# Delta rule: when the SP queue fetches the attention channels, and when the ACT queue fetches the bias bands

## The chip, the cores and the metric
The kernel runs on one NeuronCore of a Trainium2 chip. The metric is the device time of one execution in microseconds (us). Five engines take part: TensorE (PE: matmuls, and its weight loads, PEld), VectorE (DVE), ScalarE (ACT), GpSimd (POOL) and SyncE (SP), which here only issues DMAs. The core has 16 DMA engines. DMAs that SP issues run on queue q1, those that ACT issues on queue q10.

## The reference
One decoder block over 2048 tokens of width 1024. What matters here is the gated delta rule of four heads (width 128), which runs over the sequence in chunks, and the attention that follows it:

```python
def step(state, inp):
    u0_c, w_c, qg_c, kg_c, aqk_c, gl_c = inp
    u = u0_c - jnp.einsum("bhck,bhkv->bhcv", w_c, state)
    o = jnp.einsum("bhck,bhkv->bhcv", qg_c, state) + jnp.einsum("bhij,bhjv->bhiv", aqk_c, u)
    state = gl_c[..., None, None] * state + jnp.einsum("bhck,bhcv->bhkv", kg_c, u)
    return state, o
...
# attention, three dilations
s = jnp.einsum("brnqhd,brnkhd->brnhqk", qb, kk) * (dh ** -0.5)
s = s + bias.transpose(2, 0, 1)
```

A chunk's state needs the state of the chunk before, so the chunks run one after another. Around these two parts stand a conditioned norm, one projection, an output projection, a router, 32 experts and a final norm.

## The kernel before
The program runs phase by phase: projection of tokens, projection of channels (with the products of every chunk of the delta rule, stored to DRAM), `deltanet` (16 chunks of 128 tokens; stage D below), `attention`, output and routing, experts, final norm. Between phases all engines meet at a barrier. The change is in `deltanet` alone.

In `deltanet` each engine runs its own loop over the chunks, and semaphores tie the loops together. Per chunk c:

- **SP** (`load_solve`, `store`, `load_z`, `load_chain`). In turn c of its loop it issues, strictly in this order: `load_solve(c + 2)`, that is one load of `nt` (256 KB) and eight small block loads into `dz` and `dzt` (16 KB each, in rows of 128 bytes); `store(c - 1)`, which waits for `y_out_ready`, the last step of POOL for chunk c - 1; `load_z(c + 1)`; `load_chain(c + 2)`, five loads of 256 KB (`kc`, `vb`, `kg`, `qg`, `aqk`); and then, in turns 0 to 7, one attention channel block, `m.qk[:, c, :]` (1 MB, from `ch_d` into `big`, L1064). Nobody in this stage reads that block. The attention reads it after the barrier.
- **PE** runs `read_state(c)`, `sixth_z(c)`, `fifth_y(c + 1)`, `solved(c)`, `fifth_z(c + 1)`, `outputs(c)`, `sixth_y(c + 1)`. `fifth_y(c + 1)` waits for `nt_in` and `d_in`, the landing of all nine loads of `load_solve(c + 1)`. `solved(c)` gives `u` of chunk c.
- **ACT** copies `u` out of PSUM (L1186), squares and copies the outputs, and takes a root. In turns 2, 3 and 4, before all that, it issues one bias band for the attention (`bias[:, c - 2, :, :]`, 1 MB in rows of 1 KB, L1181). Nobody in this stage reads that either. ACT waits for the three bands at the stage's end.
- **DVE** masks, subtracts and forms the next state. After the next state of chunk c it runs `reciprocals(c - 1)`.
- **POOL** scales the output; its last step for chunk c - 1 waits for `reciprocals(c - 1)` and releases SP's `store(c - 1)`.

The copy of `u` on ACT happens once for each chunk. The text calls its start U(c) and uses it as the clock of the stage.

Of the kernel before, what the change touches and what calls it, by code (L numbers as in the profile page):

```python
# [11 lines left out]
P = 128  # L12
T = 2048
NT = T // P
# [9 lines left out]
NCONV = 3 * GH  # L24
AH = 8
# [3 lines left out]
NB = len(BR)  # L29
BIAS_W = 384  # L30
# [133 lines left out]
def row_bc(ap, n, offset=0):  # L164

    return bass.AP(ap.tensor, ap.offset + offset, [[0, P], [1, n]])
# [290 lines left out]
def small_blocks(ap, row0, b):  # L457

    return bass.AP(ap.tensor, ap.offset + (row0 + b) * SB * SB, [[SB, SB], [P // SB * SB * SB, GH], [1, SB]])
# [495 lines left out]
def deltanet(nc, m, a):  # L955
# [5 lines left out]
    with Room(nc, "gd") as R:  # L961
# [15 lines left out]
        gain_in, later_in, zeroed, eps_set = R.sig("gain_in", 16), R.sig("later_in", 16), R.sig("zeroed"), R.sig("eps_set")  # L977
# [6 lines left out]
        bias = m.bias[:, :].rearrange("p (n h k) -> p n h k", n=NB, h=AH)  # L984
        bias_in = R.sig("bias_in", 16)
# [5 lines left out]
        def h4(ap):  # L991
            return ap.rearrange("p (h n) -> p h n", h=GH)

        def hs(h):
            return slice(h * P, (h + 1) * P)
# [3 lines left out]

        L5, L6 = C_L5, C_L6  # L1000
        BL = 2 * (P // SB)

        with R.block() as block:
            @block.sync
            def _(sp):
                def load_solve(c):
                    b = c % 2
                    if c >= 2:
                        sp.wait_ge(*y_done.n(2 * (c - 1)))
                    sp.dma_start(nt[b][:, :], m.nt_d[c]).then_inc(*nt_in[b].inc)  # L1010
                    if c >= 2:
                        sp.wait_ge(*dd_ready.n(c - 1))
                        sp.wait_ge(*dt_ready.n(c - 1))
                    else:
                        sp.wait_ge(*zeroed.n(2))
                    for k in range(P // SB):
                        s = slice(k * SB, (k + 1) * SB)
                        sp.dma_start(h4(dz[b][s, :])[:, :, s], small_blocks(m.xb_d, c * GH * P // SB, k)).then_inc(*d_in[b].inc)
                        sp.dma_start(h4(dzt[b][s, :])[:, :, s], small_blocks(m.xtb_d, c * GH * P // SB, k)).then_inc(*d_in[b].inc)

                def load_chain(c):
                    b = c % 2
                    if c >= 2:
                        sp.wait_ge(*ks_done.n(c - 1))
                        sp.wait_ge(*r_ready.n(c - 1))
                    if c:
                        sp.dma_start(h4(kc[b][:, :]), m.ch_d[GH:2 * GH, :, c * P:(c + 1) * P].rearrange("c p n -> p c n")).then_inc(*k_in[b].inc)
                    sp.dma_start(vb[:, b, :], m.vb_d[c]).then_inc(*vb_in[b].inc)
                    if c >= 2:
                        sp.wait_ge(*ds_done.n(c - 1))  # L1030
                    sp.dma_start(kg[:, b, :], m.kg_d[c]).then_inc(*kg_in[b].inc)
                    if c >= 2:
                        sp.wait_ge(*o_done.n(c - 1))
                    sp.dma_start(qg[:, b, :], m.qg_d[c]).then_inc(*qg_in[b].inc)
                    sp.dma_start(aqk[:, b, :], m.aqk_d[c]).then_inc(*aqk_in[b].inc)

                def load_z(c):
                    b = c % 2
                    if c >= 2:
                        sp.wait_ge(*y_out_ready.n(c - 1))  # L1040
                    sp.dma_start(z[:, b, :], m.z_d[c]).then_inc(*z_in[b].inc)

                def store(c):
                    b = c % 2
                    sp.wait_ge(*y_out_ready.n(c + 1))
                    sp.dma_start(m.y_d[c], o[:, b, :]).then_inc(*out[b].inc)

                sp.dma_start(gain[:, :], row_bc(a["gdn_norm"], P)).then_inc(*gain_in.inc)
                load_chain(0)
                load_solve(1)  # L1050
                load_chain(1)
                load_z(0)
                load_z(1)
                for c in range(NT):
                    if c + 2 < NT:
                        load_solve(c + 2)
                    if c >= 1:
                        store(c - 1)
                        if c + 1 < NT:
                            load_z(c + 1)  # L1060
                    if c + 2 < NT:
                        load_chain(c + 2)
                    if c < m.NCH - NCONV:
                        sp.dma_start(m.qk[:, c, :], m.ch_d[NCONV + c]).then_inc(*later_in.inc)  # L1064
                store(NT - 1)
                sp.wait_ge(*later_in.n(m.NCH - NCONV))
                for b in range(2):
                    sp.wait_ge(*out[b].n(NT // 2))
# [27 lines left out]
            def _(pe):  # L1096
# [5 lines left out]
                def fifth_y(c):  # L1102
                    b = c % 2
                    if c:
                        pe.wait_ge(*nt_in[b].n((c + 1) // 2))
                        pe.wait_ge(*d_in[b].n((c + 1) // 2 * BL))

# [63 lines left out]
            @block.scalar  # L1171
            def _(act):
                act.wait_ge(*eps_set.n(1))
                nc.scalar.activation(nrm[:, :, :], m.ssq[:, :, :], ACT.Sqrt, bias=eps[:, :]).then_inc(*nstd_ready.inc)
                act.wait_ge(*nrm_ready.n(2))
                for c in range(NT):
                    b = c % 2
                    if 2 <= c < 2 + NB:

                        src = bass.AP(m.bias_d.tensor, (c - 2) * AH * P * BIAS_W + P - 1, [[BIAS_W - 1, P], [P * BIAS_W, AH], [1, 2 * P]])  # L1180
                        act.dma_start(bias[:, c - 2, :, :], src).then_inc(*bias_in.inc)  # L1181
                    act.wait_ge(*u_done.n(c + 1))
                    if c >= 2:
                        act.wait_ge(*ds_done.n(c - 1))
                        act.wait_ge(*o_done.n(c - 1))
                    nc.scalar.copy(u[:, b, :], ps[:, U, :]).then_inc(*u_ready.inc)  # L1186
                    act.wait_ge(*o_done.n(c + 1))
                    if c >= 2:
                        act.wait_ge(*y_out_ready.n(c - 1))
                    act.wait_ge(*out[b].n(c // 2))  # L1190
                    for h in range(GH):
                        ins = nc.scalar.activation(o2[:, hs(h)], ps[:, O + b, hs(h)], ACT.Square, scale=nrm[:, c, h:h + 1], accum_out=st[:, b, h:h + 1])
                    ins.then_inc(*osq_ready.inc)
                    nc.scalar.copy(o[:, b, :], ps[:, O + b, :]).then_inc(*o_ready.inc)
                    act.wait_ge(*osq_ready.n(c + 1))
                    nc.scalar.activation(st[:, b, :], st[:, b, :], ACT.Sqrt, bias=eps[:, :], scale=1.0 / P).then_inc(*std_ready.inc)
                act.wait_ge(*bias_in.n(NB))
# [1136 lines left out]


PHASES = (condition_and_project, project_channels, deltanet, attention, mix_and_route, experts, finish)


def block_kernel(nc, a, out):
# [3 lines left out]
    with ExitStack() as ctx:  # L2343
# [37 lines left out]
        with nc.sbuf_tensor("w_chan", [P, KD, P], F32) as m.w_chan:  # L2381
            for phase in PHASES[:2]:
                phase(nc, m, a)
        m.bias = sb("bias", [P, NB * AH * 2 * P])
        deltanet(nc, m, a)
        m.w_out = ctx.enter_context(nc.sbuf_tensor("w_out", [P, KD, D], F32))
        m.wd = m.w_out[:, :, :].rearrange("p k n -> p (k n)")
# [56 lines left out]
```

## Time and profile before

| | us |
|---|---|
| median of 3 runs (lowest, highest) | 2434.1 (2432.55, 2439.28) |
| the profiled execution, its own time | 2443.93 |
| its span, first to last instruction | 2441.8 |
| PE busy in the span | 2204.0 (90%) |
| DVE, ACT, POOL busy | 1117.0, 918.4, 384.8 |
| U(0) to U(15), the 16 copies of `u` | 979.37 to 1143.53 |

PE is busy for nearly the whole program, but in stage D it works through a chain of short matmuls with the other engines in between. There the share of PE says little. What counts is the distance from one U to the next and what PE waited for when it grew. Times in rows are microseconds from the span's start.

### The profile page before, as it was taken

The numbers are of one execution on the slowest core, as the hardware profiler recorded it, in microseconds if no ns is written. First come the engines' busy times: TensorE is split into PE (matmuls) and PEld (weight loads), VectorE is DVE, ScalarE is ACT, GpSimd is POOL, SyncE is SP. The second block draws the span as 40 slices with busy tenths as digits, with TensorE's granted clock in tenths as the row PEclk, the third lists the DMA queues.
The fourth block names the chain that finished last, engine by engine and source line by source line (L and its number), as shares of the span: only waits on it lengthen the run. The fifth ranks groups of instructions, "written<-read, shape, count | busy, mean of one in ns | idle before, by whom it ended". The sixth has DMA issues, their size and how long they took to land. (4 is left out here: it accounts for less than half of the span.)

```text
span 2441.8 us, 33277 instructions
## 1 busy us (share of the span) xinstructions
PE 2204.0 (90%) x9996; PEld 1242.2 (51%) x9997; DVE 1117.0 (46%) x2278; ACT 918.4 (38%) x2135; POOL 384.8 (16%) x320
## 2 busy tenths in 40 slices
PE   5999999999988898897999998999957998999990
PEld 2666644444454444787777776555532333333330
DVE  3344322223243652454887876687752222222223
ACT  1333121111133320222778875444313443444433
POOL 0000000000011100335333210011122222222220
PEclk8999999999999999999999999999978999999995
DMA  8444112311245552985433323545465988889737
GB/s 338 147 147 155 61 47 78 121 52 61 99 156 171 182 193 93 308 262 180 161 94 99 105 91 121 177 156 147 126 256 151 297 270 294 294 266 316 208 78 292
DMA packets 178321, 418.15 MB, mean 171 GB/s; under 512 B 41192, under 2 KB 81000, under 8 KB 162744
## 3 DMA queue, kind: packets, MB, share of 16 engines
q1 hardware_dynamic: 155944, 346.59, 41.1%
q0 software_dynamic: 13472, 45.26, 8.1%
q10 hardware_dynamic: 8816, 25.18, 2.9%
q8 instruction: 47, 0.77, 0.1%
q14 instruction: 42, 0.34, 0.0%
HBM read 296.84 MB, written 124.85 MB: 173 GB/s over the span
## 5 line engine op out<-in xcount | busy, mean ns | idle before, releaser
L2163 PE MATMUL ps<-big,bias 128*64 x672 | 301.4, 602 | 2.7 <-DVE ex_wgu L2255 1.8
L2164 PE MATMUL ps<-ex_wgu,bias 128*64 128x512 f32 x672 | 301.4, 602 | 0.0
L693 PE MATMUL ps<-big,w_chan 128*128 128x512 f32 x640 | 279.9, 597 | 3.2 <-PEq L139 3.2
L693 PE MATMUL ps<-big,pc_w 128*128 128x512 f32 x640 | 278.2, 593 | 0.0
L345 PE MATMUL ps<-cp_wt,big 128*128 128x344 f32 x768 | 225.6, 454 | 0.0
L1681 PE MATMUL ps<-w_out,mo_yt 128*128 128x512 f32 x512 | 223.7, 594 | 0.0
L693 PEld LDWEIGHTS ps<-big,w_chan 128*128 128x128 f32 x640 | 121.9, 192 | 154.4 <-issue 154.4
L693 PEld LDWEIGHTS ps<-big,pc_w 128*128 128x128 f32 x640 | 121.2, 191 | 149.3 <-issue 149.3
L345 PEld LDWEIGHTS ps<-cp_wt,big 128*128 128x128 f32 x768 | 146.0, 191 | 77.0 <-issue 4.1
L1413 PE MATMUL ps<-at_v,at_pt 128*128 128x128 f32 (+1 forms) x1200 | 183.3, 290 | 0.0
L2163 PEld LDWEIGHTS ps<-big,bias 128*64 128x64 f32 x672 | 89.6, 138 | 181.0 <-issue 181.0
L1479 ACT ACTIVATE at_p<-at_p,at_low 128x256 f32<-128x256 f32 (+1 forms) x384 | 174.0, 456 | 19.0 <-DVE at_low L1442 18.7
L2214 ACT COPY ex_wgu<-big 128x4096 f32 x42 | 151.6, 3608 | 62.6 <-SPq L2084 32.0
L1413 PEld LDWEIGHTS ps<-at_v,at_pt 128*128 128x128 f32 x1200 | 149.5, 192 | 46.4 <-issue 36.4
L2175 PE MATMUL ps<-w_out,bias 128*64 x336 | 153.2, 598 | 2.6 <-DVE mod L2239 1.5
L1681 PEld LDWEIGHTS ps<-w_out,mo_yt 128*128 128x128 f32 x512 | 96.3, 191 | 114.0 <-issue 113.7
L2176 PE MATMUL ps<-ex_wd,bias 128*64 128x512 f32 x336 | 153.2, 598 | 0.0
L1440 DVE SCALAR_TENSOR_TENSOR at_p<-ps,bias 128x512 f32<-128x512 f32 (+1 forms) x192 | 109.2, 569 | 69.2 <-PE ps L1388 69.1
L1388 PE MATMUL ps<-at_kb,at_qb 64*128 64x256 f32 (+1 forms) x768 | 119.6, 389 | 13.1 <-POOL at_kb L1374 12.1
L778 ACT COPY pc_pre<-ps 128x512 f32<-128x512 f32 x48 | 28.1, 586 | 269.2 <-PE ps L693 269.2
L2126 POOL DMA_INDIRECT acc_d<-mod,ex_to x42 | 85.4, 2034 | 211.4 <-DVE mod L2239 103.4
L853 DVE TENSOR_SCALAR pc_cv<-pc_pre,pc_wc 128x2048 f32<-128x2048 f32 x12 | 15.4, 1286 | 225.3 <-ACT pc_pre L778 225.3
(315 smaller groups left out, 3311.9 us busy)
## 6 DMA issues: line engine op xcount, KB each, us to landing
big<-in_w_gate_up SPq DMA_DIRECT2D x32, 2048.0 KB, 10.4
w_out<-in_w_down SPq DMA_DIRECT2D x32, 1024.0 KB, 6.5
cp_w<-in_w_ada SPq DMA_DIRECT2D x24, 1024.0 KB, 5.4
ch_d<-pc_cv SPq DMA_DIRECT2D x20, 1024.0 KB, 4.4
at_v<-v_d SPq DMA_DIRECT2D x27, 512.0 KB, 4.0
o_d<-at_o SPq DMA_DIRECT2D x48, 264.0 KB, 2.1
mo<-o_d SPq DMA_DIRECT2D x16, 792.0 KB
pc_qkv<-ch_d SPq DMA_DIRECT2D x16, 768.0 KB, 5.6
```

Of the source, the lines that this page charges most:

```text
L345: last = nc.tensor.matmul(ps[:, ROW_A + g, 0:THIRD], m.ht[:, k, t * P:(t + 1) * P], wt[:, k, g * THIRD:(g + 1) * THIRD], start=(k == 0), s ...
L693: last = nc.tensor.matmul(ps[:, n % 2, :], w[ch % 2][:, k, :], m.ht[:, k, g * BANK:(g + 1) * BANK], start=(k == 0), stop=(k == KD - 1))
L1388: last = nc.tensor.matmul(ps[:, 2 * (s % 2) + h, lo:2 * P], qb[r, b, s, :], kb[r, b, s, lo:], start=True, stop=True)
L1413: last = nc.tensor.matmul(ps[:, 6 + b, w], pt[:, e, h, k, :], v[:, b, k, w], start=(k == k0), stop=(k == 1))
L1440: nc.vector.scalar_tensor_tensor(p[:, s, :, lo:], ps[:, 2 * e:2 * e + 2, lo:2 * P], DH ** -0.5, bias[:, unit[0][1], 2 * s:2 * s + 2, lo:], ...
L1479: ins = nc.scalar.activation(p[:, s, h, lo:], p[:, s, h, lo:], ACT.Exp, bias=low[:, b, at:at + 1], accum_out=low[:, b, at + AH:at + AH + 1])
L1681: last = nc.tensor.matmul(ps[:, 2 + 2 * b + n, :], yt[:, b, k, :], w[:, k, n * BANK:(n + 1) * BANK], start=(k == 0), stop=(k == KD - 1))
L2163: nc.tensor.matmul(ps[0:HB, 2 + b, :], xt[:, b, k, 0:HB], wgu[:, bass.ds(at * WGU + k * 2 * DE, 2 * DE)], start=(k == 0), stop=(k == KD - 1))
L2164: last = nc.tensor.matmul(ps[HB:P, 2 + b, :], xt[:, b, k, HB:P], wgu2[:, b, k, :], start=(k == 0), stop=(k == KD - 1))
L2175: nc.tensor.matmul(ps[0:HB, 6 + c, :], hidt[:, b, k, 0:HB], wd[:, bass.ds(at * WD + (k * D + c * BANK), BANK)], start=(k == 0), stop=(k == ...
L2176: last = nc.tensor.matmul(ps[HB:P, 6 + c, :], hidt[:, b, k, HB:P], wd2[:, b, k, c * BANK:(c + 1) * BANK], start=(k == 0), stop=(k == DE // ...
L2214: nc.scalar.copy(wgu2[:, b, :, :].rearrange("p k n -> p (k n)"), wgu[:, bass.ds(at * WGU, WGU)]).then_inc(*wgu2_ready[b].inc)
```

## The change
Of the channel blocks one is issued in every second turn of SP's loop (0, 2, ..., 14) instead of one in each of the first eight turns. The three bias bands are issued by ACT ahead of chunks 9, 11 and 13 instead of chunks 2, 3 and 4. The transfers themselves, their number, sizes and queues, stay the same.

```diff
         BL = 2 * (P // SB)
+        BIAS_AT = tuple(NT - 7 + 2 * n for n in range(NB))
...
                     if c + 2 < NT:
                         load_chain(c + 2)
-                    if c < m.NCH - NCONV:
-                        sp.dma_start(m.qk[:, c, :], m.ch_d[NCONV + c]).then_inc(*later_in.inc)
+                    if c % 2 == 0:
+                        sp.dma_start(m.qk[:, c // 2, :], m.ch_d[NCONV + c // 2]).then_inc(*later_in.inc)
...
-                    if 2 <= c < 2 + NB:
-
-                        src = bass.AP(m.bias_d.tensor, (c - 2) * AH * P * BIAS_W + P - 1, [[BIAS_W - 1, P], [P * BIAS_W, AH], [1, 2 * P]])
-                        act.dma_start(bias[:, c - 2, :, :], src).then_inc(*bias_in.inc)
+                    if c in BIAS_AT:
+                        n = BIAS_AT.index(c)
+                        src = bass.AP(m.bias_d.tensor, n * AH * P * BIAS_W + P - 1, [[BIAS_W - 1, P], [P * BIAS_W, AH], [1, 2 * P]])
+                        act.dma_start(bias[:, n, :, :], src).then_inc(*bias_in.inc)
```

SP's queue in the stretch from turn 8 into turn 9, before: `load_chain(10)` ends with `kg`, `qg` and `aqk`, and `load_solve(11)` follows at once (`nt`, then the blocks of `dz` and `dzt`).

```order
L1031 DMA gd_kg<-kg_d 128x512
L1034 DMA gd_qg<-qg_d 128x512
L1035 DMA gd_aqk<-aqk_d 128x512
L1010 DMA gd_nt<-nt_d 128x512
L1018 DMA gd_dz<-xb_d 32x4x32
L1019 DMA gd_dzt<-xtb_d 32x4x32
```

The same place on SP after the change (line numbers are one higher):

```order
L1032 DMA gd_kg<-kg_d 128x512
L1035 DMA gd_qg<-qg_d 128x512
L1036 DMA gd_aqk<-aqk_d 128x512
L1065 DMA big<-ch_d 128x2048
L1011 DMA gd_nt<-nt_d 128x512
L1019 DMA gd_dz<-xb_d 32x4x32
L1020 DMA gd_dzt<-xtb_d 32x4x32
```

A channel block now stands ahead of `load_solve(11)`. The same holds in turns 10, 12 and 14 (in turn 14 no `load_solve` follows); from turns 1, 3, 5 and 7 the block is gone.

ACT's queue from chunk 8 to the copy of `u` of chunk 9, before (`gd_u` is `u`, `gd_st` the sums of squares):

```order
L1186 COPY gd_u<-ps 128x512
L1192 ACTIVATE gd_o2,gd_st<-ps,gd_nrm 128x128 x4
L1194 COPY gd_o<-ps 128x512
L1196 ACTIVATE gd_st<-gd_st,gd_eps 128x4
L1186 COPY gd_u<-ps 128x512
```

The same place on ACT after the change:

```order
L1187 COPY gd_u<-ps 128x512
L1193 ACTIVATE gd_o2,gd_st<-ps,gd_nrm 128x128 x4
L1195 COPY gd_o<-ps 128x512
L1197 ACTIVATE gd_st<-gd_st,gd_eps 128x4
L1182 DMA bias<-bias_d 128x8x256
L1187 COPY gd_u<-ps 128x512
```

The first bias band now follows the root of chunk 8; the second and third follow those of chunks 10 and 12. Before, they followed chunks 1, 2 and 3.

## Rows read from the trace of the kernel before

**Rows 1.** The page's first line.
```profile
span 2441.8 us, 33277 instructions
```

**Rows 2.** Waits in stage D: total, times, longest.
```profile
ACT gd_u L1186 <- PE ps L1099: 74.1, 16, 13.5
...
PE ps L1099 <- issue: 18.7, 7, 5.6
```

**Rows 3.** ACT in time: start, duration, line; copies of u, two bias issues.
```profile
979.37 0.59 ACT L1186 COPY gd_u<-ps 128x512 f32<-128x512 f32 x1 [13.51 <-PE ps L1099]
988.70 0.59 ACT L1186 COPY gd_u<-ps 128x512 f32<-128x512 f32 x1 [2.59 <-PE ps L1099]
994.72 0.42 ACTq L1181 DMA_DIRECT2D bias<-bias_d  x1
998.04 0.59 ACT L1186 COPY gd_u<-ps 128x512 f32<-128x512 f32 x1 [2.69 <-PE ps L1099]
...
1014.67 0.59 ACT L1186 COPY gd_u<-ps 128x512 f32<-128x512 f32 x1 [9.98 <-PE ps L1099]
1021.58 0.37 ACTq L1181 DMA_DIRECT2D bias<-bias_d  x1
1024.90 0.59 ACT L1186 COPY gd_u<-ps 128x512 f32<-128x512 f32 x1 [2.68 <-PE ps L1099]
1041.33 0.59 ACT L1186 COPY gd_u<-ps 128x512 f32<-128x512 f32 x1 [9.72 <-PE ps L1099]
1051.87 0.59 ACT L1186 COPY gd_u<-ps 128x512 f32<-128x512 f32 x1 [2.68 <-PE ps L1099]
1064.04 0.59 ACT L1186 COPY gd_u<-ps 128x512 f32<-128x512 f32 x1 [5.52 <-PE ps L1099]
...
1085.97 0.59 ACT L1186 COPY gd_u<-ps 128x512 f32<-128x512 f32 x1 [5.50 <-PE ps L1099]
1096.38 0.59 ACT L1186 COPY gd_u<-ps 128x512 f32<-128x512 f32 x1 [2.68 <-PE ps L1099]
...
1134.20 0.59 ACT L1186 COPY gd_u<-ps 128x512 f32<-128x512 f32 x1 [2.68 <-PE ps L1099]
1143.53 0.59 ACT L1186 COPY gd_u<-ps 128x512 f32<-128x512 f32 x1 [2.68 <-PE ps L1099]
```

**Rows 4.** PE in time: four starts of fifth_y, with the idle time before.
```profile
1010.88 2.04 PE L1099 MATMUL ps<-mod 128*128 128x128 f32 x8 [5.58 <-issue]
...
1037.54 2.05 PE L1099 MATMUL ps<-mod 128*128 128x128 f32 x8 [5.32 <-issue]
...
1061.98 1.13 PE L1099 MATMUL ps<-mod 128*128 128x128 f32 x8 [2.84 <-issue]
...
1083.36 1.13 PE L1099 MATMUL ps<-mod 128*128 128x128 f32 x8 [2.27 <-issue]
```

**Rows 5.** SP in time: store(4); store(6), channel block 7, last block of load_solve(10).
```profile
1047.84 0.36 SPq L1046 DMA_DIRECT2D y_d<-gd_o  x1
...
1069.49 0.36 SPq L1046 DMA_DIRECT2D y_d<-gd_o  x1
...
1072.85 0.43 SPq L1064 DMA_DIRECT2D big<-ch_d  x1
...
1078.21 0.43 SPq L1019 DMA_DIRECT2D mod<-xtb_d  x1
```

**Rows 6.** Stretches: length, busy of five engines, granted clock, DMA share, GB/s.
```profile
1020.00:1022.00 2.00, 2.00 (x19) 1.92 (x18) 0.76 (x2) 1.96 (x10) 1.84 (x2) 1.00 0.25 70
1022.00:1043.00 21.00, 15.68 (x113) 15.35 (x112) 8.20 (x21) 3.57 (x14) 7.13 (x6) 0.85 1.05 351
...
1070.00:1088.00 18.00, 15.57 (x119) 15.01 (x118) 8.83 (x23) 4.19 (x16) 7.57 (x7) 0.91 1.00 307
...
1111.00:1121.00 10.00, 10.00 (x88) 9.76 (x88) 5.95 (x16) 3.44 (x17) 5.25 (x6) 1.00 0.72 225
```

**Rows 7.** DMA queues between 960 and 1150 us: packets, MB, share of 16 engines.
```profile
q10 hardware_dynamic: 3120, 3.15, 5.6%
```

## The prediction
> **What bounds the kernel now.** I read the page first (its span, 2441.8 us [rows 1]), then the waits of stage D, the timelines of ACT, PE and SP there, and last the DMA share by stretches. PE's 90% busy over the program does not decide anything here: stage D is a chain of short steps, and its clock is U(c), the start of the copy of `u`. Rows 3 show U(0) to U(7), U(9), U(10), U(14) and U(15), and two bias issues between them. Undisturbed, a chunk takes 1143.53 - 1134.20 = 9.33 us [rows 3]. Fifteen such steps would be 140.0 us; the stage took 1143.53 - 979.37 = 164.2. So 24.2 us are lost, and the change can move little else. ACT waits for `u` 74.1 us in 16 waits; the part of it that is no ordinary step of the chain stands on PE, which waited 18.7 us in seven pieces for nothing that an engine released [rows 2]. Its large pieces are 5.58, 5.32, 2.84 and 2.27 us, each ahead of the first matmul of `fifth_y` [rows 4]. The code says what `fifth_y(c + 1)` waits for: the nine landings of `load_solve(c + 1)`. So the loss is late landings.
>
> **Why they are late.** Follow the one at 1083.36, `fifth_y(10)`. U(7) is 1064.04 [rows 3]. SP was free for `store(6)` only at 1069.49, 5.45 us later, when POOL had finished chunk 6. Then SP issued the loads of the chain, the channel block of turn 7 at 1072.85, and `load_solve(10)`, whose last block went out at 1078.21 [rows 5]. It landed some 5.2 us later: PE started at 1083.36 after 2.27 us of waiting [rows 4], and U(9) was 1085.97, 2.61 us after that [rows 3]. In sum U(9) - U(7) = 5.45 + 8.72 + 5.15 + 2.61 = 21.93 us. This is a loop over *two* chunks: U(c), the store of c - 1, the burst of turn c, `load_solve(c + 3)` at the start of turn c + 1, `fifth_y(c + 3)`, U(c + 2). It costs nothing while it stays under 2 x 9.33 = 18.66 us. Even and odd chunks have a loop each, and the two overlap in time.
>
> So I price pairs, each from its own rows [rows 3]:
> - no megabyte before the blocks: U(15) - U(14) = 9.33, so a pair is 18.66;
> - first pair: U(2) - U(0) = 18.67, with the block of turn 0 in it. That block is free, since the first turns are not yet held by a store;
> - one channel block: U(7) - U(5) = 22.71 and U(9) - U(7) = 21.93, middle 22.3;
> - one channel block and one bias band issued with it: U(3) - U(1) = 25.97 (bias at 994.72) and U(5) - U(3) = 26.66 (bias at 1021.58), middle 26.3.
>
> The bias band comes 6.0 and 6.9 us after U, just as the burst begins (its `store` came 5.45 us after U(7), and 6.51 us after U(5), at 1047.84 [rows 5]). The DMA queues had run nearly dry before such a burst: share 0.25 from 1020 to 1022 [rows 6]. So the price belongs to that pair and is not inherited from the one before. The next 21 us ran at a share of 1.05 with a mean granted clock of 0.85 [rows 6]: part of the price is that PE came back at 1.2 GHz after its long wait, with 2.05 us for eight matmuls where the shorter stalls of 2.84 and 2.27 us are followed by 1.13 [rows 4].
>
> **The change, part by part.** It removes no transfer and no instruction. What it does is to pair transfers anew.
>
> *Channel blocks in turns 0, 2, ..., 14.* Each stands ahead of the `load_solve` of an odd chunk and so lengthens only the loop of the even chunks. Turn 0 is free as before. Turns 2, 4 and 6 make U(4) - U(2), U(6) - U(4) and U(8) - U(6) a channel pair each: 3 x 22.3 = 66.9 us. That the odd turns are now empty does not help these three pairs: in the pair from U(7) the burst of turn 8 already had no block, and it still took 21.93. The block of turn 14 has no `load_solve` behind it; behind it stands only the last store, over 9 us later. Free.
>
> *Bias bands ahead of chunks 9, 11 and 13.* ACT issues them after the roots of chunks 8, 10 and 12, so about 6 to 7 us after U(8), U(10), U(12). That is the burst of turns 8, 10 and 12, the ones with a channel block. So U(10) - U(8), U(12) - U(10) and U(14) - U(12) are pairs with both: 3 x 26.3 = 78.9 us. The third band is issued over 20 us before the stage ends, so the attention does not wait for it.
>
> *The last step.* A chunk after a stall takes more than 9.33: U(4) - U(3) = 10.23, U(6) - U(5) = 10.54, U(10) - U(9) = 10.41 [rows 3]. Inside pairs this is contained. U(15) - U(14) stands alone: 10.4.
>
> *Sum.* U(0) to U(15) = 18.7 + 66.9 + 78.9 + 10.4 = 174.9 us, against 164.2 before: **10.7 us longer**. The point is that before, the stalls of the even loop ran beside those of the odd loop: the second band, between the two shown, cost no pair of its own, and seven channel blocks shared two loops. After, all six disturbed pairs stand in a row on one loop. Against the profiled execution's own 2443.9 us this gives 2454.6; that execution was 9.8 us over the median, so I move the median: 2434.1 + 10.7 = **2444.8 us**.
>
> What a band costs by itself in a pair is 26.3 - 22.3 = 4.0 us. Its transfers took 5.6% of 190 us over three bands [rows 7], 3.5 us each of all 16 engines, so nearly the whole transfer lands on the path. The Trainium skill (DMA: Bandwidth & Descriptors, "Anatomy of one DMA — SWDGE (gpsimd) path") fits a transfer as about 2.0 us plus bytes over 436e9 per second, measured on GpSimd's queue. By that page one MiB would hold the engines 2.4 us, the three bands 7.2 us instead of 12, and the sum would be an estimated 5.9 us longer. The measured 3.5 us decides against it.
>
> **Bounds.** From below: the only thing that cannot be argued away is the work of the DMA engines. A chunk without a megabyte is 10 us x 0.72 = 7.2 us of work, two chunks and one block 18 x 1.00 = 18.0 us [rows 6]. That is less than 18.66, so a channel pair could be free; with a band it is 21.5, 2.8 over. That gives 140.0 + 3 x 2.8 = 148.4 us, 15.8 less than before. From above: every pair at its dearer row, 18.67 + 3 x 22.71 + 3 x 26.66 + 10.4 = 177.2, 13.0 more; and if the odd loop also stalls, because the band of turn 9, 11 or 13 is still in transfer when its blocks come, another 1 us for each of six pairs, 19 more.
>
> **The rivals.**
> - *Only bandwidth counts (faster).* The change spreads 11 MB over the stage; if a burst with room behind it drains in time, the times are those of the lower bound, 2434.1 - 15.8 = 2418 us. For it: the share was 1.05 through the early burst, and after the change the first half is never saturated. Against it: the loop from U(7) had an empty turn behind it and gained 0.8 us only. It decides if the six disturbed pairs lose less than (24.2 - 1.1) / 6 = 3.9 us each on average; my rows say 3.6 and 7.6. Chance with its milder forms, 0.13.
> - *Half relieved (same).* A block alone costs 2 us because the SP queue issues faster into empty rings, and a band 4 more: 3 x 2 + 3 x 6 + 1.1 = 25.1, 0.9 more, 2435 us. For it: the chain's slack without a megabyte is not seen, and both channel pairs of the rows stand in the wake of the bands. Chance 0.30.
> - *The forecast, 7 to 14 us slower*: 0.51.
> - *Worse*: the odd loop stalls too, or the clock falls in each of the six pairs, +19 us, 2453 us. Chance 0.06.
>
> **How the numbers follow.** A difference of 0.3%, 7.3 us, is about what a measurement of this kernel can tell from no change. The forecast at 10.7 lies over it by 3.4 us, so some of its chance falls inside: faster 0.12, same 0.34, slower 0.54. Range: from 2426 (the bandwidth case half realised) to 2454 (the odd loop too). The likeliest case's own range is 2441 to 2448.
>
> **What would show it.** In the profile after, stage D from U(0) to U(15) near 175 us; U(3) - U(2) back to 9.3; the stalls before `fifth_y` only ahead of odd chunks' blocks, at U(4), U(6), U(8) small (2 to 3 us) and at U(10), U(12), U(14) large (over 5 us) with granted clock falling behind them; the last step 10.4. I am wrong if the pairs to U(4), U(6), U(8) take under 20 us, or those to U(10), U(12), U(14) under 24: then a burst with an empty turn behind it costs less than the same burst in a full row.

## The result, and the profile after

| | before | after |
|---|---|---|
| median (lowest, highest; 9 runs each) | 2436.3 (2432.02, 2441.31) | 2448.32 (2440.75, 2453.86) |
| ratio, 95% interval | | 1.0051 (1.0037 to 1.0065) |
| the profiled execution, its own time | 2443.93 | 2449.72 |
| U(0) to U(15) in it | 164.16 | 175.91 |

The change makes the kernel 12.0 us slower; 10.7 were forecast, with 2444.8 as the time. In the profiled executions stage D grew by 11.75 us. The profiled execution of before was a long one for its kernel (2443.93 us against a median of 2436.3), so its whole span, 2441.8 against 2447.6 us, shows only half of the difference.

The 11.75 us divide into two parts. Two stretches, from U(0) to U(15), first before and then after (length, busy of the five engines, PE first, granted clock, DMA share, GB/s):

```profile
979.37:1143.53 164.16, 146.74 (x1192) 142.77 (x1191) 87.89 (x224) 41.49 (x165) 66.72 (x59) 0.95 0.83 265
...
977.55:1153.46 175.91, 151.08 (x1192) 147.17 (x1191) 87.92 (x224) 41.50 (x165) 66.83 (x60) 0.92 0.77 244
```

By the profile's count PE ran the same 1192 matmuls in both. It sat idle for 17.42 us before and 24.83 after, 7.4 us more, and the same matmuls kept it busy for 4.3 us longer, at a mean granted clock of 0.92 instead of 0.95. So somewhat over a third of the loss is slower matmuls, and the rest is waiting.

The copies of `u` on ACT after the change, with the three bias issues (start, duration, line; the sixteen copies are U(0) to U(15)). They answer to [rows 3].

```profile
977.55 0.59 ACT L1187 COPY gd_u<-ps 128x512 f32<-128x512 f32 x1 [13.44 <-PE ps L1100]
...
996.22 0.59 ACT L1187 COPY gd_u<-ps 128x512 f32<-128x512 f32 x1 [2.68 <-PE ps L1100]
1005.56 0.59 ACT L1187 COPY gd_u<-ps 128x512 f32<-128x512 f32 x1 [2.68 <-PE ps L1100]
1019.87 0.59 ACT L1187 COPY gd_u<-ps 128x512 f32<-128x512 f32 x1 [7.66 <-PE ps L1100]
...
1041.66 0.59 ACT L1187 COPY gd_u<-ps 128x512 f32<-128x512 f32 x1 [4.61 <-PE ps L1100]
...
1065.17 0.59 ACT L1187 COPY gd_u<-ps 128x512 f32<-128x512 f32 x1 [7.37 <-PE ps L1100]
1071.94 0.42 ACTq L1182 DMA_DIRECT2D bias<-bias_d  x1
...
1091.55 0.59 ACT L1187 COPY gd_u<-ps 128x512 f32<-128x512 f32 x1 [9.65 <-PE ps L1100]
1098.77 0.37 ACTq L1182 DMA_DIRECT2D bias<-bias_d  x1
...
1116.55 0.59 ACT L1187 COPY gd_u<-ps 128x512 f32<-128x512 f32 x1 [7.81 <-PE ps L1100]
1123.23 0.37 ACTq L1182 DMA_DIRECT2D bias<-bias_d  x1
...
1143.10 0.59 ACT L1187 COPY gd_u<-ps 128x512 f32<-128x512 f32 x1 [9.90 <-PE ps L1100]
1153.46 0.59 ACT L1187 COPY gd_u<-ps 128x512 f32<-128x512 f32 x1 [2.68 <-PE ps L1100]
```

The long waits stand in the last bracket, and all of them at even chunks: U(4) 7.66, U(6) 4.61, U(8) 7.37, U(10) 9.65, U(12) 7.81, U(14) 9.90, where an ordinary one is 2.68. U(3) comes 9.34 us after U(2). Before, that step was 16.63.

The starts of `fifth_y` that PE waited for, after the change, answering to [rows 4] (start, duration, idle time before it in brackets):

```profile
1016.08 2.05 PE L1100 MATMUL ps<-gd_dz,gd_nt 128*128 128x128 f32 x8 [3.25 <-issue]
1039.60 1.13 PE L1100 MATMUL ps<-gd_dz,gd_nt 128*128 128x128 f32 x8 [1.93 <-issue]
...
1062.24 1.18 PE L1100 MATMUL ps<-gd_dz,gd_nt 128*128 128x128 f32 x8 [3.83 <-issue]
1087.76 2.05 PE L1100 MATMUL ps<-gd_dz,gd_nt 128*128 128x128 f32 x8 [5.24 <-issue]
1113.53 1.27 PE L1100 MATMUL ps<-gd_dz,gd_nt 128*128 128x128 f32 x8 [4.18 <-issue]
1139.31 2.04 PE L1100 MATMUL ps<-gd_dz,gd_nt 128*128 128x128 f32 x8 [5.50 <-issue]
```

Before, the four long ones all read `mod`, the buffers of even chunks, on the way to an odd U; now all six read `gd_dz`, those of odd chunks, on the way to an even U. One loop carries everything. The waits on the way to U(4), U(6) and U(8) are 3.25, 1.93 and 3.83 us where the prediction said 2 to 3, and those to U(10), U(12) and U(14) are 5.24, 4.18 and 5.50 where it said over 5.

One turn of the loop, the pair from U(8) = 1065.17 to U(10) = 1091.55, on SP (the store that opens the burst, the channel block, the last small block of `load_solve(11)`):

```profile
1071.23 0.36 SPq L1047 DMA_DIRECT2D y_d<-gd_o  x1
...
1074.99 0.46 SPq L1065 DMA_DIRECT2D big<-ch_d  x1
...
1080.40 1.81 SPq L1020 DMA_DIRECT2D gd_dzt<-xtb_d  x1
```

From U(8) to the store it is 6.06 us, to the last block 9.17, to PE's start at 1087.76 7.36, and to U(10) 3.79: 26.38 in sum. The prediction's pair without a band had 5.45 + 8.72 + 5.15 + 2.61 = 21.93. The last block's landing (2.2 us more) and PE's way from there to U (1.2 us more, with the slow matmuls in it) make most of the difference.

Two stretches of the same execution (length, busy of the five engines, granted clock, DMA share, GB/s), answering to [rows 6]. One is the double burst of turns 8 and 9, the other the gap behind it:

```profile
1072.00:1092.00 20.00, 14.76 (x110) 14.32 (x109) 8.27 (x21) 3.79 (x14) 7.37 (x7) 0.88 1.03 327
...
1093.00:1098.00 5.00, 5.00 (x43) 5.00 (x42) 2.75 (x8) 0.78 (x5) 1.01 (x2) 0.91 0.02 5
```

The queues are full for 20 us and then empty for 5, while SP waits until 1098.06 for the store that opens the next burst. So inside the burst the late blocks compete for full DMA engines, and over the whole pair there is room, but only after those blocks have landed.

### The profile page after: what moved, and what is told of

Read it like the earlier page. It is cut to its first block and busy times, and to the rows that moved or that the text cites. A ratio compares the mean times of both kernels' runs of the same rounds, so it can differ in the third digit from the quotient of the medians.

```text
span 2447.6 us, 33277 instructions
## 1 busy us (share of the span) xinstructions
PE 2204.5 (90%) x9996; PEld 1243.5 (51%) x9997; DVE 1116.5 (46%) x2278; ACT 918.4 (38%) x2135; POOL 386.0 (16%) x320
```

## The experiments

U(0) to U(15) below is read as above, from each kernel's profile. Ratios are against the kernel before, run on the same chip. The change was not timed beside these kernels (e9 is one execution of it), so a comparison with it goes by each kernel's distance to the before beside it.

| kernel | us | ratio (95%) | U(0) to U(15) |
|---|---|---|---|
| e1 channel blocks alternate, bands early | 2439.79 | 1.0020 (1.0008 to 1.0032) | 166.37 |
| e2 blocks early, bands late | 2435.75 | 1.0005 (0.9992 to 1.0018) | 159.15 |
| e3 the change, bands one chunk earlier | 2435.72 | 1.0007 (0.9992 to 1.0021) | 165.32 |
| e4 the change, blocks behind load_solve | 2425.93 | 0.9968 (0.9955 to 0.9980) | 150.39 |
| e5 all at the end | 2439.90 | 1.0018 (1.0003 to 1.0033) | 140.29 |
| e6 all behind load_solve, spread | 2420.46 | 0.9931 (0.9912 to 0.9949) | 145.89 |
| e7 before, blocks behind load_solve | 2431.04 | 0.9975 (0.9961 to 0.9988) | 156.74 |
| e8 before, profiled again | 2433.6 (one run) | | 159.24 |
| e9 after, profiled again | 2449.96 (one run) | | 172.52 |

**The halves of the change, e1 and e2.** Each kernel has one of the two edits.

```diff
e1, against before:
-                    if c < m.NCH - NCONV:
-                        sp.dma_start(m.qk[:, c, :], m.ch_d[NCONV + c]).then_inc(*later_in.inc)
+                    if c % 2 == 0:
+                        sp.dma_start(m.qk[:, c // 2, :], m.ch_d[NCONV + c // 2]).then_inc(*later_in.inc)
e2, against the change:
-                    if c % 2 == 0:
-                        sp.dma_start(m.qk[:, c // 2, :], m.ch_d[NCONV + c // 2]).then_inc(*later_in.inc)
+                    if c < m.NCH - NCONV:
+                        sp.dma_start(m.qk[:, c, :], m.ch_d[NCONV + c]).then_inc(*later_in.inc)
```

> Channel blocks in turns 0, 2, ..., 14 as in the change, bias bands in turns 2 to 4 as before. Theory of the two loops (each pair of chunks has its price, even and odd chunks overlap): U(0) to U(2) 18.7, U(2) to U(4) with block and band about 26, the bands of the odd loop hidden beside it, then five pairs with a block at the 23 us that the changed kernel showed, last step 10.4: 170 us from U(0) to U(15), so 6 us more than the kernel before, and 6 us less than the change. Rival, bandwidth alone: spreading the blocks relieves the queues, 10 to 15 us less than the kernel before.

> Channel blocks in turns 0 to 7 as before, bias bands ahead of chunks 9, 11, 13 as in the change. Loop theory: four pairs with a block from U(1) to U(9), both loops side by side at 22.3; then three pairs with a band alone at about 22.5 (18.66 plus the 4 us of a band); last step 10.4: 166 us, 2 us more than before, no difference that can be told. Rival, bandwidth alone: 10 us less than before.

e1 is 5.1 us slower than the kernel before, where 6 were expected; its stage took 166.37 us where I had 170. Spreading the blocks alone is a loss, although it takes a megabyte out of every second turn. e2 cannot be told from before, as expected of it (2 us; 1.1 measured); its stage took 159.15 us where I had 166. Its pairs with a block, both loops at it, are 20.6 to 21.6 us, cheaper than the 22.3 I had from the rows. There both loops stall, at every chunk from U(3) to U(8), and a pair is no dearer than in the change, where only one loop stalls: that is the overlap, seen directly. Its three pairs from U(8) to U(14), with a band and no block, took 23.07, 20.59 and 22.32 us: a band alone costs 3.3 us on average over 18.66. Together the halves lose more than the sum of each: 5.1 and 1.1 against 12.0, though the 5.8 us between them are hardly more than the three intervals leave open. The theory puts that down to the overlap, which the next kernel tests.

**The two loops, e3.**

```diff
-        BIAS_AT = tuple(NT - 7 + 2 * n for n in range(NB))
+        BIAS_AT = tuple(NT - 8 + 2 * n for n in range(NB))
```

> The change, but with the bands one chunk earlier, ahead of chunks 8, 10 and 12: a band then meets the burst of an odd turn, which has no channel block. Same transfers, same spacing. Loop theory: the even loop pays 23 us for a block, the odd loop about 22.5 for a band, at the same time: 18.7 + 6 x 23 + 10.4 = 167 us, 9 us less than the change. Rival: a band costs its 4 us wherever it is issued, because the engines have the same work: 176 us, as the change.

Only the chunk of the bands moved, by one. The kernel is back at the time of before (2435.72, 1.1 us over the before beside it, where the change was 12.0 over its own), with a stage of 165.32 us where 167 was expected and 176 by the rival. The transfers and the spacing are those of the change, so their total work does not decide. What does is where the bands fall: on the other loop, and thereby also in another burst than the channel block. e3 alone does not separate these two; the pairs of e2 speak for the loops. The profiled execution was the longest of e3, 2449.22 us, but its stage is 10.6 us shorter than that of the change with nearly the same span (2447.1 against 2447.6 us), so the excess lies outside the stage. The ACT timeline of e3 around the second band, which is issued 6.0 us after U(9):

```profile
1069.05 0.59 ACT L1187 COPY gd_u<-ps 128x512 f32<-128x512 f32 x1 [6.25 <-PE ps L1100]
1079.12 0.58 ACT L1187 COPY gd_u<-ps 128x512 f32<-128x512 f32 x1 [2.69 <-PE ps L1100]
1085.13 0.39 ACTq L1182 DMA_DIRECT2D bias<-bias_d  x1
1094.69 0.58 ACT L1187 COPY gd_u<-ps 128x512 f32<-128x512 f32 x1 [8.93 <-PE ps L1100]
1104.02 0.59 ACT L1187 COPY gd_u<-ps 128x512 f32<-128x512 f32 x1 [2.69 <-PE ps L1100]
1110.03 0.37 ACTq L1182 DMA_DIRECT2D bias<-bias_d  x1
1116.41 0.59 ACT L1187 COPY gd_u<-ps 128x512 f32<-128x512 f32 x1 [5.75 <-PE ps L1100]
```

U(8), U(10) and U(12) are the lines with the long waits; the odd ones between wait 2.69. The odd loop's 22 us run out inside the time that the even loop has lost already. One band is not hidden whole, the second: U(8) to U(10) took 25.64 us, with a wait of 4.70 us ahead of `fifth_y` at 1091.08. It was issued at 1085.13, before the last small block of the even loop (1085.67). The first and the third band (1062.17, 1110.03) were issued just after the last small block (1062.00, 1108.48), and PE waited 2.68 and 2.38 us there. That fits a band that shares the DMA engines with the late blocks; no run moves this band alone. The later two pairs took 21.72 and 22.76.

**The place on the queue, e4 and e7.** In both a channel block is issued behind `load_solve` instead of ahead of it.

```diff
e4, against the change:
                     if c + 2 < NT:
                         load_solve(c + 2)
+                    if c % 2:
+                        sp.dma_start(m.qk[:, c // 2, :], m.ch_d[NCONV + c // 2]).then_inc(*later_in.inc)
...
-                    if c % 2 == 0:
-                        sp.dma_start(m.qk[:, c // 2, :], m.ch_d[NCONV + c // 2]).then_inc(*later_in.inc)
e7, against before:
                     if c + 2 < NT:
                         load_solve(c + 2)
+                    if 1 <= c <= m.NCH - NCONV:
+                        sp.dma_start(m.qk[:, c - 1, :], m.ch_d[NCONV + c - 1]).then_inc(*later_in.inc)
...
-                    if c < m.NCH - NCONV:
-                        sp.dma_start(m.qk[:, c, :], m.ch_d[NCONV + c]).then_inc(*later_in.inc)
```

> The change, but each channel block is issued one place later on SP's queue, behind the load_solve of the next turn instead of ahead of it. Theory, the price is that of the block standing ahead of the small blocks on one queue: a channel pair falls to about 19.5 us and a pair with a band to about 22.7: 18.7 + 58.5 + 68 + 10.4 = 156 us, 20 us less than the change and 8 less than before. Rival, the DMA engines' work sets the pairs: 176 us, no difference to the change.

> The kernel before with one thing moved: each channel block is issued behind the load_solve of the next turn (turns 1 to 8) instead of ahead of it; bands as before. Theory, place on the queue: pairs with blocks alone fall from 22 to about 20.4 (two turns of 10.2 us of engine work), the pairs with bands from 26 to about 24.5: U(0) to U(15) about 155 us and the program 6 to 9 us faster than before, although nothing is spread. Rival: the place helps only in the change's spread schedule, because in eight full turns the engines have no room: within 3 us of before.

e4 is 8.7 us faster than before and so some 21 us faster than the change, with the same spacing of the same transfers. PE's waits ahead of `fifth_y` in e4 on the way to U(10), U(12) and U(14), the pairs with a band:

```profile
1071.48 1.13 PE L1100 MATMUL ps<-gd_dz,gd_nt 128*128 128x128 f32 x8 [1.03 <-issue]
...
1092.30 1.13 PE L1100 MATMUL ps<-gd_dz,gd_nt 128*128 128x128 f32 x8 [2.01 <-issue]
...
1114.01 1.13 PE L1100 MATMUL ps<-gd_dz,gd_nt 128*128 128x128 f32 x8 [1.48 <-issue]
```

Where the change waited 5.24, 4.18 and 5.50 us for block and band, e4 waits 1.03, 2.01 and 1.48, and its eight matmuls take 1.13 us each time. The stage, 150.39 us where 156 was expected, again divides into waiting and slower matmuls:

```profile
975.16:1125.55 150.39, 140.10 (x1192) 135.75 (x1191) 87.82 (x224) 41.40 (x166) 66.76 (x60) 1.00 0.90 286
```

PE is busy 11.0 us less than in the change and idle 14.5 us less, so a good part of what the place gives back is the clock, 1.00 instead of 0.92. U(4) to U(6) and U(6) to U(8) took 20.06 and 19.81 us here, U(8) to U(10) 21.18. A small stall now also stands on the other loop: PE waited 1.24, 1.00 and 1.35 us on the way to U(5), U(7) and U(9). e7 is 4.8 us faster than before, less than the 6 to 9 expected, with a stage of 156.74 us (155 expected). Its two pairs with the bands, U(2) to U(4) and U(3) to U(5), still took 26.29 and 26.35 us where 24.5 was expected: there the place of the block gave nothing. The overall gain is clear of noise, so the place pays in the crowded schedule too, and more in the spread one.

**The floor and a better kernel, e5 and e6.** e5 issues the eight blocks ahead of SP's last store and the three bands behind ACT's last chunk. e6 sends all eleven through SP:

```diff
e6, against the change:
+                late = {t: n for n, t in enumerate((0, 2, 4, 5, 7, 8, 10, 11, 13, 14, 15))}
+
+                def load_later(c):
+                    n = late.get(c)
+                    if n is None:
+                        return
+                    if n < m.NCH - NCONV:
+                        sp.dma_start(m.qk[:, n, :], m.ch_d[NCONV + n]).then_inc(*later_in.inc)
+                        return
+                    n -= m.NCH - NCONV
+                    src = bass.AP(m.bias_d.tensor, n * AH * P * BIAS_W + P - 1, [[BIAS_W - 1, P], [P * BIAS_W, AH], [1, 2 * P]])
+                    sp.dma_start(bias[:, n, :, :], src).then_inc(*bias_in.inc)
...
                     if c + 2 < NT:
                         load_solve(c + 2)
+                    load_later(c)
...
-                    if c % 2 == 0:
-                        sp.dma_start(m.qk[:, c // 2, :], m.ch_d[NCONV + c // 2]).then_inc(*later_in.inc)
...
-                        act.dma_start(bias[:, n, :, :], src).then_inc(*bias_in.inc)
```

> No megabyte during the chunks: all eight channel blocks are issued by SP behind the last turn, ahead of the last store, and the three bands by ACT behind its last chunk. Loop theory: U(0) to U(15) = 15 x 9.33 = 140 us with no stall ahead of fifth_y; the transfers then take some 34 us of the engines behind U(14), so the stage ends about where it did before: within 5 us of the kernel before. Rival: part of the 24 us lost in stage D has another cause (the loop is over 18.66 us without any block), then U(0) to U(15) stays over 145 us.

> All eleven megabytes go through SP's queue, each behind a load_solve: channel blocks in turns 0, 2, 4, 5, 7, 8, 10, 11, bands in turns 13, 14, 15, the last two where no load of a later chunk follows. Theory of the place on the queue: each costs 0.5 to 1 us, U(0) to U(15) 145 to 150 us, the program 14 to 19 us faster than before. Rival, the engines' work: 16 turns at 7.2 us and 33 us for the megabytes are 148 us, but if a block costs its 3 us wherever it stands, 165 us and no difference to before.

e5 settles the premise: U(0) to U(15) is 140.29 us. Two stretches of e5, up to the last chunk and behind it:

```profile
965.00:1110.00 145.00, 140.81 (x1188) 137.03 (x1188) 88.00 (x221) 39.31 (x155) 64.27 (x56) 0.98 0.76 232
1110.00:1150.00 40.00, 9.47 (x79) 8.81 (x77) 7.20 (x18) 4.94 (x21) 9.19 (x8) 0.69 0.85 319
```

The loss of stage D is the megabytes, to within 0.3 us. From U(0) to U(15):

```profile
978.03:1118.32 140.29, 139.20 (x1192) 135.29 (x1191) 87.86 (x224) 41.49 (x165) 66.79 (x59) 1.00 0.74 229
```

PE is busy for 139.20 of the 140.29 us, so the undisturbed step of 9.33 us is almost entirely PE's own work at full clock. The share of PE, which the text ahead of the prediction set aside, does say something here: it is what remains when nothing is late. Moved to the end, the megabytes lie bare on the path instead, and the kernel is 5.9 us slower, a little outside the 5 expected. e6 is the fastest of all, 2420.46 us, 13.6 less than the before beside it (ratio 0.9931), with a stage of 145.89 us in the forecast band of 145 to 150; the gain is just short of the 14 to 19 expected. The expectation's estimate from the engines' work, 148 us, lies in the same band, so e6 refutes only that a block costs 3 us wherever it stands. It also changes several things at once (the queue of the bands, their turns, the spacing), and no run says what each is worth.

**How steady is a pair's price, e8 and e9.** Both kernels unchanged, profiled again.

> The kernel before, unchanged, profiled a second time: how much does a pair's price differ between executions? If the prices belong to the schedule, U(0) to U(15) comes within 3 us of 164.2 and the stalls stand at the same chunks; if they are chance, the stalls move and the sum differs by more.

> The changed kernel, unchanged, profiled a second time: U(0) to U(15) within 3 us of 175.9, all six stalls at U(4), U(6), ..., U(14) and none at an odd chunk, if the prices belong to the schedule.

In e9 the six stalls stand at U(4), U(6), ..., U(14) again, and the sum is 172.52 against 175.91, 3.4 us less where 3 were allowed. In e8 the stalls stand at the same odd chunks too, but they are smaller, and the sum is 159.24 against 164.16: 4.9 us, outside the 3 that I had allowed. PE's waits in e8:

```profile
1006.06 2.05 PE L1099 MATMUL ps<-mod 128*128 128x128 f32 x8 [5.02 <-issue]
...
1031.86 2.04 PE L1099 MATMUL ps<-mod 128*128 128x128 f32 x8 [3.92 <-issue]
...
1054.32 1.13 PE L1099 MATMUL ps<-mod 128*128 128x128 f32 x8 [1.49 <-issue]
...
1075.79 1.13 PE L1099 MATMUL ps<-mod 128*128 128x128 f32 x8 [2.08 <-issue]
```

The schedule sets where a stall is; its size differs from one execution to the next: a wait by up to 1.4 us in before and 1.5 in the change, a pair by up to 2.0 (U(5) to U(7), 22.71 and 20.73). The means of two executions each are 161.7 and 174.2 us, 12.5 apart, close to the 12.0 timed. In the second executions, too, the stage's growth (13.28 us) is 7.7 us of idle PE and 5.6 of slower matmuls.

## Why the prediction was right, step by step

| part | forecast | first profile | second |
|---|---|---|---|
| U(0) to U(2) | 18.7 | 18.67 | 18.84 |
| to U(8), three pairs with a block | 66.9 | 68.95 | 65.59 |
| to U(14), three with block and band | 78.9 | 77.93 | 78.03 |
| last step | 10.4 | 10.36 | 10.06 |
| sum | 174.9 | 175.91 | 172.52 |

- **The loop over two chunks**: the stalls stood at the even chunks alone once the blocks stood in even turns alone, and they did so again in e9; in e2 both loops stalled at once at no more than the price of one; e3 moved three bands onto the other loop and won back the loss within the intervals. e5, without any megabyte, ran at 9.33 us a chunk, which gives the floor and not the loop.
- **A block ahead of the small blocks is the cause, not its bytes.** e4 shows it: the same bytes with the same spacing, on the other side of `load_solve`, 21 us less. The rival of bandwidth alone is refuted for the change: e1 was slower where it wanted a gain. It may have a part of the truth in e4 and e6, where pairs fall to some 20 us and not to 18.66: the DMA share over e4's stage is 0.90, against 0.77 in the change. No run shows that this is what is left.
- **The price of a pair, 22.3 and 26.3.** In the change the blocks' pairs were 23.65, 21.79 and 23.51 us, those with a band 26.38, 25.00 and 26.55. Right on average; a single one is off by up to 1.4 us, and by 1.6 in the second execution. By e2 a band alone costs 3.3 us, and with a block it costs about the 4.0 of the forecast or less (77.93 - 68.95 over three pairs is 3.0; in the second execution it is 4.1). The prices came from one execution of before. Taken in the same way from e8 they are 21.1 and 25.6 us, and the sum is 168.9 against 159.24, 9.7 longer: the difference hardly hangs on which execution is read, the stage's own time does.
- **The rate in the Trainium skill** (DMA: Bandwidth & Descriptors, "Anatomy of one DMA — SWDGE (gpsimd) path") gave the prediction an estimated 5.9 us longer, from the part of that fit that goes by bytes. The change measured 12.0, and 2.4 us a band is under every price of a band measured here (3.0, 3.3 and 4.1 us). With the 2.0 us of the same fit counted, a band would be an estimated 4.4 us and the whole 11.9 longer, so the time does not decide against the page, only against leaving that part out. No run here shows whether it applies to ACT's queue.
- **The free ones** were free. The block of turn 14 was issued at 1150.29, and from U(15) to the attention's first copy, on POOL, it is 12.56 us in both kernels (1156.09 - 1143.53 before, 1166.02 - 1153.46 after). SP around it (start, duration of issue):

```profile
1149.43 0.34 SPq L1047 DMA_DIRECT2D y_d<-gd_o  x1
1149.81 0.43 SPq L1042 DMA_DIRECT2D gd_z<-z_d  x1
1150.29 0.44 SPq L1065 DMA_DIRECT2D big<-ch_d  x1
```

- **What was mis-sized** is the time of before. The sum set 174.9 against the 164.2 of one profiled execution; a second one has 159.24. The 10.7 us are low by 1.3; against the mean of the two stages of before, 161.7, the same forecast would read 13.2, high by 1.2. One profiled execution does not give the term any better. The absolute time, 2444.8 for 2448.32, carries that 1.3 and the 2.2 us by which the before of the later runs lay over the first median.
- **The half relieved case**, which had 0.30, had no wake to point to: the pairs of the change, without bands before them, cost as much as those in the wake of the bands (22.98 us on average and 21.86 in e9, against 22.3 in the rows and 21.1 in e8). In e2, where both loops had a block in every turn, a pair took 20.6 to 21.6 us, which is nearer to this case than to 22.3; why a block costs less there stays open.

## What to carry to other kernels

A bulk transfer with no hurry should stand on a queue directly *behind* the last load that somebody will wait for, not ahead of it; that was worth 21 us in the spread schedule and 4.8 in the crowded one, where spreading the same transfers cost 12. Before moving a load, find the loop it lies on (which wait opens the burst, which landing ends it, how many turns it spans) and what runs beside it: here two disturbances on loops that overlap cost little more than one, and the same two in a row on one loop cost nearly twice. Work that must be late anyway can go into the turns where the next loads have run out: the block of turn 14 was free, and e6, the fastest kernel, puts two bands there.

## What the runs showed of the hardware

PE did not always return slow from a wait. In the change the matmuls took 2.05 us for eight right after waits of 3.25 and 5.24 us, but 1.18 and 1.27 after 3.83 and 4.18 us; there the slow ones came one group later. In e7, on the other hand, a wait of only 2.65 us was followed by eight matmuls in 2.05 us, so the length of the wait alone does not say what follows it. The three groups behind the row of 1113.53 shown above:

```profile
1114.60 1.92 PE L1100 MATMUL ps<-gd_r,gd_tt 128*128 128x128 f32 x8
1116.30 1.77 PE L1100 MATMUL ps<-gd_yy,gd_dzt 128*128 128x128 f32 x8
1117.91 1.06 PE L1100 MATMUL ps<-gd_dzt,gd_yy 128*128 128x128 f32 x8
```

In the ten microseconds that begin 1.3 to 2.2 us ahead of the matmuls that waited, the granted clock is 0.83 here and for the wait of 3.83 us, 0.66 for those of 3.25, 5.24 and 5.50 us, and 1.00 for the one of 1.93 us. Three of these stretches:

```profile
1014.00:1024.00 10.00, 7.92 (x45) 7.95 (x46) 2.32 (x4) 0.59 (x1) 0.70 (x1) 0.66 0.67 200
1038.00:1048.00 10.00, 8.40 (x73) 8.27 (x73) 4.62 (x11) 2.31 (x10) 3.41 (x4) 1.00 0.64 192
...
1112.00:1122.00 10.00, 8.47 (x61) 8.50 (x62) 3.44 (x9) 0.90 (x3) 0.55 (x1) 0.83 0.68 202
```

So part of a pair's price is decided by where the fall of the clock meets the chain: U(2) to U(4) with a wait of 3.25 us took 23.65, and U(4) to U(6) with 1.93 took 21.79, of which 1.32 us are the wait and 0.54 the rest. Over the whole stage the slower matmuls are 4.3 of the 11.75 us between the first two profiles and 5.6 of 13.28 between the second two (ends of matmuls are modelled in the profile, so these are estimates). No run holds the clock still, so what the change would cost without its falls is not measured.
